# One layer of a hybrid diffusion backbone on one core: new orders of work for TensorE, VectorE and ScalarE in the state steps, the row scale on ScalarE alone, the positions added by VectorE

## The reference

```python
def rms_norm(x, g):
    y = x * lax.rsqrt(jnp.mean(x * x, axis=-1, keepdims=True) + RMS_EPS)   # RMS_EPS = 1e-6
    return y * g

def step(state, inp):                       # RWKV-7, per head, 64 x 64 state, one token
    r_t, k_t, v_t, w_t, kk_t, b_t = inp
    sa = jnp.einsum('bhvk,bhk->bhv', state, -kk_t)
    state = (state * w_t[:, :, None, :] + sa[..., None] * b_t[:, :, None, :]
             + v_t[..., None] * k_t[:, :, None, :])
    return state, jnp.einsum('bhvk,bhk->bhv', state, r_t)

def trunk_layer(x, cond, s0, p):
    sh1, sc1, g1, sh2, sc2, g2 = adaln_mod(cond, p['ada_w'], p['ada_b'])
    h = rms_norm(x, p['norm1_g']) * (1 + sc1) + sh1
    z = h @ p['w_in']                       # 1024 x 2816
    y_rwkv, s_new = rwkv7_bidir(z[..., :SHIFT_COLS], z[..., SHIFT_COLS:SHIFT_COLS + LORA_G], s0, p)
    y_conv = conformer_conv(z[..., SHIFT_COLS + LORA_G:], p)       # depthwise, width 31
    x = x + g1 * (jnp.concatenate([y_rwkv, y_conv], axis=-1) @ p['w_out'])
    h = rms_norm(x, p['norm2_g']) * (1 + sc2) + sh2
    x = x + g2 * hier_moe(h, p)             # 32 experts, top 1 of 4 groups, top 2 of 8 in it
    return x, s_new

xs = x_sample + grid_pos_embed(rows, x_sample.dtype)[None]        # positions: sample tokens only
y_prompt, y_sample = rms_norm(xp, final_norm_g), rms_norm(xs, final_norm_g)
```

## Time and profile before

| | us |
|---|---|
| median of 3 runs | 1071.83 |
| the runs | 1071.83, 1067.16, 1073.94 |
| the profiled execution | 1072.89 |
| its span | 1071.2 |
| PE busy | 905.6 (85% of the span) |
| DVE busy | 585.8 (55%) |
| ACT busy | 291.9 (27%) |
| POOL busy | 74.0 (7%) |

### The profile page before, as it was taken

One profiled execution on the slowest core, in us unless ns is written; L12 is line 12 of the kernel. 1 busy time (PEld: TensorE's weight loads), 2 busy tenths in 40 slices (PEclk: granted clock), 3 DMA queues, 4 the chain that ended last, 5 costly groups with the idle time before them and its releaser, 6 DMA issues.

```text
span 1071.2 us, 17424 instructions
## 1 busy us (share of the span) xinstructions
PE 905.6 (85%) x6856; PEld 547.9 (51%) x6856; DVE 585.8 (55%) x1193; ACT 291.9 (27%) x510; POOL 74.0 (7%) x78
## 2 busy tenths in 40 slices
PE   2999988998998798788795899995699797998786
PEld 2566444565666576566774764453333342443232
DVE  5239999854536777777765165667433132332225
ACT  4230110240463825556531244113110000000003
POOL 0100000131000000000000000000101111011023
PEclk9899988998987759585586699997599899999899
DMA  9951642342100200200105738311889999998954
GB/s 354 338 220 59 241 184 105 124 177 89 21 2 2 29 4 11 22 2 13 20 6 58 293 150 310 138 40 79 345 350 421 419 420 419 420 420 330 377 223 194
DMA packets 75443, 198.93 MB, mean 186 GB/s; under 512 B 42015, under 2 KB 44481, under 8 KB 61155
## 3 DMA queue, kind: packets, MB, share of 16 engines
q1 hardware_dynamic: 65988, 175.30, 44.6%
q0 software_dynamic: 7456, 17.09, 4.3%
q10 hardware_dynamic: 1919, 5.44, 1.3%
HBM read 182.78 MB, written 23.40 MB: 192 GB/s over the span
## 4 chain that ended last, share of the span: by engine, by line
PE 49%; DVE 15%; DMA 10%; ACT 6%; issue 3%; SPq 1%; DVEq 0%; ACTq 0%; POOLq 0%
PE bank L2375 9%; PE bank L582 8%; DMA arena<-in_expert_w_up 7%; PE bank L1663 6%; PE bank L2396 4%; DVE arena L1040 2%; PE bank L1293 2%; PE bank L1353 2%; PE bank L1350 2%; PE bank L1280 1%; ACT arena L916 1%; PE bank L1379 1%; DMA arena<-winv 1%; PE bank L1305 1%; DVE arena L1137 1%
## 5 line engine op out<-in xcount | busy, mean ns | idle before, releaser
L582 PE MATMUL bank<-arena 128*128 128x320 f32 x704 | 212.1, 456 | 2.4 <-ACT arena L410 2.4
L582 PEld LDWEIGHTS bank<-arena 128*128 128x128 f32 x704 | 136.7, 199 | 79.5 <-issue 31.3
L2375 PE MATMUL bank<-arena 128*64 128x512 f32 (+2 forms) x496 | 124.1, 650 | 19.1 <-DMA arena<-in_expert_w_up 18.2
L1040 DVE SCALAR_TENSOR_TENSOR arena<-arena 128x655 f32<-128x655 f32 x116 | 104.6, 902 | 4.4
L2375 PEld LDWEIGHTS bank<-arena 128*64 128x64 f32 (+2 forms) x496 | 45.5, 149 | 96.0 <-issue 94.7
L2478 DVE TENSOR_TENSOR arena<-arena,bank 128x256 f32<-128x256 f32 x16 | 6.8, 422 | 124.9 <-ACT arena L2437 124.9
L1663 PE MATMUL bank<-arena 128*128 128x512 f32 x160 | 70.6, 595 | 0.0
L2396 PE MATMUL bank<-arena 128*64 128x512 f32 (+2 forms) x248 | 60.4, 614 | 9.4 <-DVE arena L2481 9.4
L2437 ACT ACTIVATE arena<-bank 128x256 f32<-128x256 f32 x16 | 6.2, 385 | 196.8 <-PE bank L2375 196.8
L2134 POOL DMA_INDIRECT arena<-tokens_for_experts,arena x17 | 17.2, 1015 | 521.9 <-DVE arena L2085 512.2
L1663 PEld LDWEIGHTS bank<-arena 128*128 128x128 f32 x160 | 29.6, 189 | 34.8 <-issue 34.6
(11 more groups left out here) (363 smaller groups left out, 1356.6 us busy)
## 6 DMA issues: line engine op xcount, KB each, us to landing
arena<-in_expert_w_gate SPq DMA_DIRECT2D x33, 1024.0 KB, 14.8
arena<-in_expert_w_up SPq DMA_DIRECT2D x33, 1024.0 KB, 20.0
arena<-in_expert_w_down SPq DMA_DIRECT2D x33, 1024.0 KB, 21.1
arena<-in_ada_w SPq DMA_DIRECT2D x12, 2048.0 KB, 10.2
arena<-in_w_in SPq DMA_DIRECT2D x22, 512.0 KB, 4.3
arena<-expert_rows SPq DMA_DIRECT2D x10, 512.0 KB, 7.3
arena<-in_w_out SPq DMA_DIRECT2D x1, 4096.0 KB, 14.9
arena<-modrows SPq DMA_DIRECT2D x6, 512.0 KB, 9.5
```

The costliest lines, as they stand in the source:

```text
L582: mm = nc.tensor.matmul(psum[4 + 2 * (n % 2) + half][:, 0:HALF], wring[:, n % NWIN, k], hT[:, k, half * HALF:(half + 1) * HALF], start=(pa ...
L1040: chain(nc.vector.scalar_tensor_tensor(acc, src, w, acc, ALU.mult, ALU.add))
L2375: mm = nc.tensor.matmul(psum[2 + n % 2][r, :], xeT[:, n % 2, c, r], gu[:, :, c, :], start=(c == 0), stop=(c == KD - 1))
```

## The change

1. The lists of PE, ACT and DVE in `ORDER` are new. The events are the same, except for `place` below. Up to the last event before X.0.0, which is the projection's part, PE's list is the same as before. ACT's is too, and DVE's differs there only by the `place` events.
2. The row scale stays on ACT: the squares are taken of x / 32 and summed (so that the sum is the mean square), and the logarithm, with the epsilon as its bias, and the exponential of minus one half of it follow. DVE's two small instructions per tile and the root go. The epsilon is kept in one column, `rms_eps`, set once by DVE in the front.
3. `preload_act_table_set("natural_log_exp_and_others")` loads one table that holds the logarithm and the exponential: at the head of ACT's work in the front, at the head of each `logn` (ahead of its wait for the norm), and at the head of the end stage. The number of table loads on ACT falls from 31 to 21; in the projection and the state steps it falls from 20 (5 at L944, 5 at L945, 7 at L926, 3 at L951) to 13.
4. The positions of the 4 sample tiles are added by DVE, as events `place.1` to `place.4`: place.1 between z.14 and kn.0, place.2 between z.16 and gram0.0, place.3 between z.18 and inv4.0, place.4 between z.19 and shift_k.1. GpSimd still issues the loads and the store, and waits for DVE between them.

```diff
...
         small = keep.take(32)
+        rms_eps = small[:, 31:32]
         lorab = keep.take(2, DR)
...
         s_modcol = sem("mod_columns_ready")
-        s_posadd, s_xstat = sem("position_added"), sem("square_sum_ready")
-        s_var, s_std, s_xn = sem("variance_ready"), sem("deviation_ready"), sem("tokens_normed")
+        s_posadd = sem("position_added")
+        s_std, s_xn = sem("row_scale_ready"), sem("tokens_normed")
         s_xT = sem("tokens_transposed")
...
                     act.wait_ge(s_posadd, i)
-                chain.announce(nc.scalar.activation(sqr, xt[:, i], ACT.Square, accum_out=small[:, i:i + 1]),
-                               s_xstat, i + 1)
+                chain(nc.scalar.activation(sqr, xt[:, i], ACT.Square, scale=D ** -0.5, accum_out=small[:, i:i + 1]))
...
             def deviation(i):
-                act.wait_ge(s_var, i + 1)
-                nc.scalar.activation(small[:, 8 + i:9 + i], small[:, i:i + 1], ACT.Sqrt).then_inc(s_std, 1)
+                chain(nc.scalar.activation(small[:, 8 + i:9 + i], small[:, i:i + 1], ACT.Ln, bias=rms_eps))
+                nc.scalar.activation(small[:, 16 + i:17 + i], small[:, 8 + i:9 + i], ACT.Exp, scale=-0.5).then_inc(s_std, 1)
...
+            nc.scalar.preload_act_table_set("natural_log_exp_and_others")
             square_sum(0)
...
             dve, chain = nc.vector, Chain(nc.vector, d_self)
+            chain(nc.vector.memset(rms_eps, RMS_EPS))
             chain(nc.vector.memset(condP, 0.0))
...
                 x = xt[:, i]
-                dve.wait_ge(s_xstat, i + 1)
-                chain.announce(nc.vector.tensor_scalar(small[:, i:i + 1], small[:, i:i + 1], 1.0 / D, RMS_EPS,
-                                                       ALU.mult, ALU.add), s_var, i + 1)
                 if i + 2 < TILES:
...
                 dve.wait_ge(s_std, i + 1)
-                chain(nc.vector.reciprocal(small[:, 16 + i:17 + i], small[:, 8 + i:9 + i]))
                 chain.announce(nc.vector.tensor_scalar(x, x, small[:, 16 + i:17 + i], None, ALU.mult), s_xn, i + 1)
...
-                   "X.0.0 turn_v1.1 T.0.0 turn_v0.1 turn_v3.1 Y.0.0 S.0.0 turn_v2.1 gram0.1 X.0.1 bonus0.1 T.0.1 gram1.1 "
...
-                   "scan0.0 z.13 shift_k.0 scan1.0 norm1.0 norm0.0 z.14 kn.0 kp0.0 kp1.0 z.15 kp2.0 ar0.0 ar1.0 bk0.0 "
...
+                   "merge_z1.0 X.0.0 turn_v0.1 T.0.0 turn_v2.1 S.0.0 gram0.1 X.0.1 Y.0.0 turn_v3.1 T.0.1 bonus0.1 turn_v1.1 S.0.1 "
...
+                    "norm0.0 z.14 place.1 kn.0 kp0.0 kp1.0 z.15 kp2.0 ar0.0 ar1.0 bk0.0 shift_v.0 bk1.0 rk.0 z.16 place.2 gram0.0 "
...
         s_cst = [sem(f"conv_tile_stored{b}") for b in range(2)]
-        s_placest = sem("placed_tokens_stored")
+        s_placed, s_placest = sem("tokens_placed"), sem("placed_tokens_stored")
...
-        def pool_mix(chain):
+        def pool_mix():
...
                 pool.dma_start(pos_in, pos[(i - 1) * P:i * P, :]).then_inc(s_sl, 16)
-                pool.wait_ge(s_sl, 16 * 8 + 32 * i)
-                chain(nc.gpsimd.tensor_tensor(tok_in, tok_in, pos_in, ALU.add))
+                pool.wait_ge(s_placed, i)
                 pool.dma_start(placed[(i - 1) * P:i * P, :], tok_in).then_inc(s_placest, 16)
...
                 elif ev == "logn":
-
+                    nc.scalar.preload_act_table_set("natural_log_exp_and_others")
                     for h in range(2):
...
                                            s_cacc, j + 1)
+                    continue
+                if ev == "place":
+                    dve.wait_ge(s_sl, 16 * 8 + 32 * u)
+                    chain.announce(nc.vector.tensor_tensor(tok_in, tok_in, pos_in, ALU.add), s_placed, u)
                     continue
...
                 i = WTILES[q]
-                dve.wait_ge(s_xstat, TILES + q + 1)
-                chain.announce(nc.vector.tensor_scalar(small[:, i:i + 1], small[:, i:i + 1], 1.0 / D, RMS_EPS,
-                                                     ALU.mult, ALU.add), s_var, TILES + q + 1)
                 dve.wait_ge(s_std, TILES + q + 1)
-                chain(nc.vector.reciprocal(small[:, 16 + i:17 + i], small[:, 8 + i:9 + i]))
...
-                chain.announce(nc.scalar.activation(xsq, x2[:, i], ACT.Square, accum_out=small[:, i:i + 1]),
-                             s_xstat, TILES + q + 1)
-                act.wait_ge(s_var, TILES + q + 1)
-                chain.announce(nc.scalar.activation(small[:, 8 + i:9 + i], small[:, i:i + 1], ACT.Sqrt), s_std, TILES + q + 1)
+                chain(nc.scalar.activation(xsq, x2[:, i], ACT.Square, scale=D ** -0.5, accum_out=small[:, i:i + 1]))
+                chain(nc.scalar.activation(small[:, 8 + i:9 + i], small[:, i:i + 1], ACT.Ln, bias=rms_eps))
+                chain.announce(nc.scalar.activation(small[:, 16 + i:17 + i], small[:, 8 + i:9 + i], ACT.Exp, scale=-0.5),
+                               s_std, TILES + q + 1)
                 if q == TILES - 1:
...
                 y = ya[:, i]
-                dve.wait_ge(s_xstat, 2 * TILES + i + 1)
-                chain.announce(nc.vector.tensor_scalar(small[:, i:i + 1], small[:, i:i + 1], 1.0 / D, RMS_EPS,
-                                                     ALU.mult, ALU.add), s_var, 2 * TILES + i + 1)
                 dve.wait_ge(s_std, 2 * TILES + i + 1)
-                chain(nc.vector.reciprocal(small[:, 16 + i:17 + i], small[:, 8 + i:9 + i]))
                 chain.announce(nc.vector.scalar_tensor_tensor(y, x2e[:, i], small[:, 16 + i:17 + i], fgain,
...
             act = nc.scalar
+            nc.scalar.preload_act_table_set("natural_log_exp_and_others")
             for i in range(TILES):
                 act.wait_ge(s_xf, i + 1)
-                chain.announce(nc.scalar.activation(fsq, x2e[:, i], ACT.Square, accum_out=small[:, i:i + 1]),
-                             s_xstat, 2 * TILES + i + 1)
-                act.wait_ge(s_var, 2 * TILES + i + 1)
-                chain.announce(nc.scalar.activation(small[:, 8 + i:9 + i], small[:, i:i + 1], ACT.Sqrt), s_std, 2 * TILES + i + 1)
+                chain(nc.scalar.activation(fsq, x2e[:, i], ACT.Square, scale=D ** -0.5, accum_out=small[:, i:i + 1]))
+                chain(nc.scalar.activation(small[:, 8 + i:9 + i], small[:, i:i + 1], ACT.Ln, bias=rms_eps))
+                chain.announce(nc.scalar.activation(small[:, 16 + i:17 + i], small[:, 8 + i:9 + i], ACT.Exp, scale=-0.5),
+                               s_std, 2 * TILES + i + 1)
...
             pool_front()
-            pool_mix(chain)
+            pool_mix()
             pool_experts(chain)
...
```

## The result

The change takes 1059.12 us in the median of 4 runs, against 1072.88 for the kernel before on the same chips; the ratio is 0.9884, with a 95% interval of 0.984 to 0.9929. Timed again later, beside another kernel, it was 0.9906 (0.9874 to 0.9937). The forecast was 1043.4: the kernel is faster by 12 us, not by 28.

What follows compares the result with a forecast made beforehand. Experts were taken as bound by weights, state steps by what stands between X, T and S with no engine full. Terms -1.7 - 9.0 - 15 + 0 - 2.7 = -28.4 gave 1044.5, adjusted to the median 1043.4 us; range 1029 to 1060.

Steps and rivals of the forecast that it cites:

- C: State steps: the new lists shorten what stands between a step's X, T and S; -15 us, bounds 0 and -24.
- the walk: State steps: new order followed with the rows' durations, each instruction starting when inputs and engine are free; -24 us in all.
- the six tenths: State steps: the share of the -24 us taken as forecast, -15, because following the order by row durations is optimistic.
- three sources that could be checked: State steps: unit 1's inverse over 2 us earlier, unit 4's table load off the path, its pair_y to merge_y -4.3.
- Rival 4: State steps: PE's clock rises too with fewer pauses; -9 us more, C at -20, 1029 us; chance 0.07.
- Rival 1: State steps give nothing, as one stall often hides another; -13.4 us in all, 1058.4 us; chance 0.14.
- A: Front: table load moved to ACT's head, small DVE instructions gone from the last tile's way; -1.7 us, bounds 0 and -2.1.
- D: Output stage: row scales lie beside PE's matmuls, so 0 us; uncovered, one tile's 0.4 us.
- B: Projection: additions off GpSimd and fewer table loads shorten two PE waits and lift the clock; -9.0 us, bounds -4 and -10.
- E: End: table load moved ahead of the stage, a small DVE pair per tile gone; -2.7 us, bounds -1 and -3.
- Rival 3: State steps slower: S and X wait on DVE behind one more preparatory instruction; C +25.6 us, 1084 in all; chance 0.06.
- Rival 5: ACT: a table switch costs more than its row; by rows 1043.4 us again, by the skill page 1035; chance 0.02.

Runs made afterwards that it cites:

- the mixed lists: The change, but with the old order on PE, ScalarE and VectorE for the steps of units 1 and 3: 1059.81 us, ratio 0.9901 to the kernel before.

## Why the prediction was wrong, point by point

**C failed, and with it the sum.** It said -15 and the traces say 0: 279.2 us before, 279.5 and 280.1 in two profiles of the change (283.9 with its lists alone), 279.2 to 280.8 with the old ones in six, with and without the other parts. The step that failed is the walk, in the words of the prediction one that "keeps" PE's clock, and the six tenths taken of it for that. It was wrong in two ways.

First, it found too many pauses. It had 24 us of them, of which 15 were taken, and 9.8 went; with PE as fast as before C would have been -9.8. Of its three sources that could be checked, the inverse of unit 1 came as said (8.8 us for 11.3), and unit 4's pair_y to merge_y in part (8.9 us for 11.7, where 7.4 was expected). The second, the table load ahead of unit 4's kn, did not: the preload came 0.02 us behind a sigmoid, so that it covered no wait, and two more loads stand between it and the exponential that kn reads, for which DVE now waits 4.14 us and not 1.40 (the line at 508.34 above).

Second, and this took the rest, the durations of a row were taken at the level at which that row had run. PE paused less and was busy 10.1 us longer with the same instructions, since more of them (the 128-wide transpositions and norms above all) now run at 1.2 GHz: 166.1 us of busy time there for 147.1. The prediction read the mean of 0.63 to 0.74 as a mixture and then did not ask which instructions lie in which part of it. Rival 4 even let the clock rise with fewer pauses; no rival let the freed time be filled by PE at the lower level. Rival 1 gave the right time, 1058.4, and that is luck: its reason, one stall behind another, is there in part (X's waits for the state and kn's for the exponential), but the pauses still fell by 9.8 us, and A and D, which it takes as forecast, came out otherwise in the profile.

**B held.** Forecast -9.0, measured -10.7 in the profile (327.85 - 317.26, and 0.1 lost ahead of it). Both slow DVE rows went to 1.54 and 1.23, the wait of 1.93 went whole, 0.18 of the 3.84 was left where 0.6 was expected, and the clock stayed at 1.00, where 0.93 was reckoned with. Run alone, the positions brought 0.3% and the one table 0.5%. Behind three of the `place` additions PE does not wait. The fourth did, in the way that the prediction named as a danger: its load had not landed, DVE waited 4.25 us for it ahead of shift_k.1, and PE then waited 1.79 us for the squares that hang on this shift, at a place where it had not waited before:

```profile
279.67 1.23 DVE L1039 TENSOR_TENSOR arena<-arena 128x1024 f32<-128x1024 f32 x1 [4.25 <-DMA arena<-table_positions]
```
```profile
284.11 1.12 PE L1276 MATMUL bank<-arena 128*128 128x512 f32 x2 [1.79 <-ACT arena L927]
```

That addition stood 13 us behind the one before it (266.54), and in that time the store of the tile before and the next load had to follow each other. The prediction took over 10 us between two places as enough; between the first two additions it was 19 us, and there DVE did not wait.

**A held up to a point and was then lost to the clock in this execution.** The modulation's first matmul came 1.56 us earlier (forecast 1.7). Before, its 32 rows took 3.64 us:

```profile
29.71 3.64 PE L549 MATMUL bank<-arena 128*32 128x512 f32 x32 [0.42 <-DVE arena L490]
```

After, they took 5.32, at a granted clock of 0.68 where it had been 1.00:

```profile
28.15 5.32 PE L547 MATMUL bank<-arena 128*32 128x512 f32 x32 [0.34 <-DVE arena L488]
...
37.46 0.78 PE L580 MATMUL bank<-arena 128*128 128x320 f32 x2 [2.11 <-ACT arena L411]
```

With the old lists, whose front is the same code, the clock was 1.00 and the same rows are:

```profile
28.05 3.64 PE L547 MATMUL bank<-arena 128*32 128x512 f32 x32 [0.34 <-DVE arena L488]
...
35.68 4.61 PE L580 MATMUL bank<-arena 128*128 128x320 f32 x8 [2.12 <-ACT arena L411]
```

Of the 13 profiles with the new front, four have 5.3 us at 0.68, and PE had paused for 1.33 to 1.37 us shortly ahead of it; nine have 3.64 at 1.00, behind a pause of 0.46 to 1.06. These nine start the first z matmul at 35.15 to 36.58 (mean 35.9), the four others at 37.24 to 37.48. But the four profiles with the old front, the same code each time, lie at 36.28 to 38.83 (mean 37.2). So A is worth some 1.4 us where the clock stays up and nothing where it falls, and the 37.34 of the kernel before is itself one draw of several.

**D** was 0 by forecast; the profiles of before and after show -1.8 and -1.05 lost. The other kernels settle this: they put it to the profile of before and not to the row scale. From X.4.0 to the last router matmuls it is 128.2 us before and 129.05 to 129.2 in the three others that keep the old row scale, and 127.1 to 130.0 in those with the new one. The last logits' matmuls took 2.09 us before, at a granted clock of 0.75, and 2.94 after, at 0.57 (from the last router transposition to the routing's first matmul); they took 2.92 to 2.96 in the same three others. So D was 0 as far as these profiles can tell.

**E held**: -2.3 for -2.7, the same 15.5 us in every kernel that has the row scale on ScalarE, and 17.8 to 18.3 in those without.

**Rival 3** (slower, by DVE's longer work between X and S) did not happen to the whole, but its mechanism is in the waits of X for L1218, up from 4.4 to 10.3 us, and the longest of them is at the very place that it named, kn.4 and kp1.4 between X.2.5 and S.2.5.

**Rival 5** took from the Trainium skill, ScalarE: Activation LUTs, section What ACT_TABLE_LOAD costs, that a switch is 1.28 us of load and another 1.38 of drain. The load is 1.28 us in the rows, the drain is not in them, also where ScalarE had just been at work: before the change, a load follows right behind the logarithm that ends at 225.45 (224.39 + 1.06), and the exponential within 0.02 us behind the load. So for this kernel a switch costs what its row says.

```profile
225.46 1.28 ACT L945 ACT_TABLE_LOAD   x1
226.76 1.06 ACT L945 ACTIVATE arena<-arena 128x1024 f32<-128x1024 f32 x1
```

**What stays open** is why the sum of the four units is 280 us with either set of lists and with the mixed one, where single units move by 9 us, and why the clock is down for 186 us of the steps after the change and 177 before, with fewer pauses. The experiment with the mixed lists shows only that a unit's length does not belong to its own list.

## What to carry to other kernels

Where the granted clock of a stretch is a mixture, split it before costing a reordering: time saved from a wait in a low-clock part has to pay for the matmuls that move into it, at what they cost at the lower level (here 429 ns for 280 for a 128x128 row, and only 183 for 172 for a 16x16 one). A fall in pauses with an equal rise in busy time, at equal instruction counts, is the sign. And parts that end a wait on a nearly full engine (here an addition taken off GpSimd, a table load put ahead of a wait) pay as costed or better, while lists that move waits about in a chain of three engines are first to be tried alone against the old ones.

## What the runs showed of the hardware that was not expected

- Extra matmuls of 128 columns in the pauses brought the mean clock of the steps from 0.67 to 0.85, with two per place to 0.75, with one to 0.71. The same number with 32 columns left it at 0.64, with PE busy for 99.2 us on them for 86.9 on the wide ones, and pausing for 16.9 us for 29.5.
- PE was full, 8.00 of 8 us (436 to 444), with 182 of its 241 rows 16x16 products, and still at 0.50.
- At a given level 32 columns cost nearly as much as 128: 278 and 402 ns a row for 287 and 440.
- An extra matmul took PE 0.69 us between the 16x16 and 32x32 ones (44.1 us for 64), all at the lower level, and 0.34 behind X and T (86.9 us for 256), most of them at the upper one.
- The same front code ran its 32 modulation rows in 3.64 us in nine executions and in 5.3 in four, so a single profile can't tell a gain of 1.7 us there.
- A table load started within 0.02 us behind the activation before it, and the next activation within 0.02 us behind the load.
